# Turning attention probabilities by halves of 64 queries on two row halves of TensorE

## The reference, cut to what matters

```python
def masked_softmax(s, mask):
    s = jnp.where(mask, s, NEG)
    p = jax.nn.softmax(s, axis=-1)
    return jnp.where(mask, p, 0.0)

s = jnp.einsum('bhqd,bhkd->bhqk', qi, kh).astype(jnp.float32) * scale
s = s + ci[..., None] - c_h[:, :, None, :]
p = masked_softmax(s, key_pos[None, :] <= t[:, None])
return jnp.einsum('bhqk,bhkd->bhqd', p.astype(vh.dtype), vh)
```

## Time and profile before

| | |
|---|---|
| median of 3 runs | 1459.34 us (1457.41 to 1459.77) |
| the profiled execution: time | 1457.6 us |
| its span | 1455.8 us |
| TensorE busy | 1423.5 us, 98% |
| weight loads (beside TensorE) | 924.4 us, 63% |
| VectorE busy | 936.0 us, 64% |
| ScalarE busy | 859.1 us, 59% |
| fox loop and nsa loop | from 976 to 1015 us and from 1260 to 1407 us of the span |

### The profile page before, as it was taken

How to read it: one execution, slowest core, us unless ns; L and a number is a source line. 1 busy time by engine, 2 the same in 40 slices (tenths; PEclk the granted TensorE clock), 3 DMA queues, 4 the chain that set the end, 5 groups by cost and what they waited for, 6 DMA issues and landing times.

```text
span 1455.8 us, 24918 instructions
## 1 busy us (share of the span) xinstructions
PE 1423.5 (98%) x10148; PEld 924.4 (63%) x10148; DVE 936.0 (64%) x2086; ACT 859.1 (59%) x1184; POOL 64.9 (4%) x151
## 2 busy tenths in 40 slices
PE   7999999999999999999999999999999999899998
PEld 4444477555568548667588874746695855466677
DVE  6731565888688666555677624578667336788864
ACT  6654356777654765454473554557655557677863
POOL 0000000000000100000010000100100000000000
PEclk9999999999999999999999999999999999999999
DMA  6333322223232433333332333230223433200002
GB/s 194 97 106 100 103 87 88 66 76 120 75 128 89 142 108 102 129 126 102 102 101 75 117 93 111 89 116 3 67 88 116 137 105 98 72 2 1 2 4 99
DMA packets 128563, 132.32 MB, mean 91 GB/s; under 512 B 9961, under 2 KB 125329, under 8 KB 128321
## 3 DMA queue, kind: packets, MB, share of 16 engines
q1 hardware_dynamic: 126000, 121.56, 26.1%
q0 software_dynamic: 2448, 9.17, 1.9%
HBM read 128.58 MB, written 2.10 MB: 90 GB/s over the span
## 4 chain that ended last, share of the span: by engine, by line
PE 90%; DVE 4%; ACT 3%; issue 1%; DMA 1%; SPq 0%; POOL 0%; DVEq 0%; ACTq 0%
PE bank L740 14%; PE bank L742 14%; PE bank L741 14%; PE bank L793 8%; PE bank L795 8%; PE bank L794 8%; PE bank L992 3%; PE bank L1009 3%; PE bank L975 3%; DVE wring L1987 1%; PE bank L919 1%; PE bank L937 1%; PE bank L971 1%; PE bank L1167 1%; PE bank L873 1%
## 5 line engine op out<-in xcount | busy, mean ns | idle before, releaser
L740 PE MATMUL bank<-xT,whigh 128*128 128x512 f16 x952 | 360.8, 379 | 1.6 <-DVE wring L1987 1.6
L741 PE MATMUL bank<-xT,whigh 128*128 128x512 f16 x952 | 360.8, 379 | 0.0
L742 PE MATMUL bank<-xT,wring 128*128 128x512 f16 x952 | 360.8, 379 | 0.0
L1987 DVE SCALAR_TENSOR_TENSOR wring<-wring,wsc,whigh 128x2048 f16<-128x2048 f32 (+2 forms) x106 | 245.2, 2313 | 136.1 <-ACT whigh L1356 135.5
L1356 ACT ACTIVATE whigh<-wring,wsc 128x2048 f16<-128x2048 f32 (+2 forms) x106 | 209.0, 1972 | 108.8 <-DVE wsc L1890 88.2
L1373 ACT ACTIVATE whigh<-wring 128x2048 bf16<-128x2048 f32 (+2 forms) x106 | 199.1, 1878 | 91.2 <-DMA wring<-in_w_down 26.9
L793 PE MATMUL bank<-whigh,slab 128*128 128x256 f16 x800 | 218.0, 273 | 1.8 <-DVE wring L1987 1.3
L795 PE MATMUL bank<-whigh,slab 128*128 128x256 f16 x800 | 218.0, 273 | 0.0
L794 PE MATMUL bank<-wring,slab 128*128 128x256 f16 x800 | 218.0, 273 | 0.0
L740 PEld LDWEIGHTS bank<-xT,whigh 128*128 128x128 f16 x952 | 93.4, 98 | 113.8 <-issue 2.7
L742 PEld LDWEIGHTS bank<-xT,wring 128*128 128x128 f16 x952 | 93.1, 98 | 112.3
(11 more groups left out here) (333 smaller groups left out, 2245.3 us busy)
## 6 DMA issues: line engine op xcount, KB each, us to landing
wring<-in_w_in SPq DMA_DIRECT2D x27, 1024.0 KB, 5.1
wring<-in_w_up SPq DMA_DIRECT2D x16, 1024.0 KB, 5.4
wring<-in_w_down SPq DMA_DIRECT2D x16, 1024.0 KB, 5.1
wring<-in_even_w_in SPq DMA_DIRECT2D x14, 1024.0 KB, 5.3
wring<-in_odd_w_in SPq DMA_DIRECT2D x14, 1024.0 KB, 5.1
wring<-in_w_a SPq DMA_DIRECT2D x4, 1024.0 KB, 5.3
wring<-in_w_out SPq DMA_DIRECT2D x4, 1024.0 KB, 5.1
wring<-in_even_w_out SPq DMA_DIRECT2D x4, 1024.0 KB, 5.1
```

The costliest lines, as they stand in the source:

```text
L740: pe.matmul(bank, wh[:, k, wcol:wcol + width], xh[:, k, :], start=k == 0, stop=False)
L741: pe.matmul(bank, wh[:, k, wcol:wcol + width], xl[:, k, :], start=False, stop=False)
L742: mm = pe.matmul(bank, wl[:, k, wcol:wcol + width], xh[:, k, :], start=False, stop=k == KC - 1)
L1987: dve.scalar_tensor_tensor(low_of(i)[:, :, 0:m], loaded(i)[:, :, 0:m], wsc[:, n:n + 1], high_of(i)[:, :, 0:m], ALU.mult, ALU.subtract).the ...
```

## The change

For every block of 128 queries by 128 keys, two transposes stand where one stood. Each takes 64 queries: half k = 0 on partitions 0 to 63, half k = 1 on 64 to 127, with the 64x64 corner of the identity on the same partitions. Half k goes to bank `TPB[k]`, where the blocks of both heads follow each other in pieces of 64 columns; before, each head had its bank. ScalarE's copy puts them in order, so that `xT` holds for each head all 128 queries of a block side by side. A head's part begins at e times the step's width, no longer at a multiple of 512. TensorE waits once for the scaling of both heads, where it waited for each in turn.

```diff
-        def turned_probs(i, e):
-            return xT[:, 2 * (i % TURNED_SLOTS) + e, :]
+        def turned_pair(i, w):
+            return xT[:, 2 * (i % TURNED_SLOTS):2 * (i % TURNED_SLOTS) + 2, :].rearrange("p a n -> p (a n)")[:, 0:2 * w]
+
+        def turned_probs(i, e, w):
+            return turned_pair(i, w)[:, e * w:e * w + w]
...
+                        pe.wait_ge(s_(n + "_pn"), n_(n + "_pn", 2 * s + 2))
+                        w = width(steps[s][2])
                         for e in range(2):
-                            pe.wait_ge(s_(n + "_pn"), n_(n + "_pn", 2 * s + e + 1))
-                            for j in range(width(steps[s][2]) // P):
-                                mm = pe.transpose(TPB[e][:, j * P:(j + 1) * P], probs(s, e, SEQ)[:, j * P:(j + 1) * P], ident[:, :])
+                            for j in range(w // P):
+                                for k in range(2):
+                                    rows = slice(k * HD, k * HD + HD)
+                                    c = (e * w + j * P) // 2
+                                    mm = pe.transpose(TPB[k][:, c:c + HD], probs(s, e, SEQ)[rows, j * P:(j + 1) * P], ident[rows, rows])
...
-                                    mm = pe.matmul(ob[e][:, t * P:(t + 1) * P], A.v(2 * m + e, b, j), turned_probs(s, e)[:, c + j * P:c + (j + 1) * P],
+                                    mm = pe.matmul(ob[e][:, t * P:(t + 1) * P], A.v(2 * m + e, b, j), turned_probs(s, e, width(parts))[:, c + j * P:c + (j + 1) * P],
...
-                        c = 2 * (s % TURNED_SLOTS)
                         act.wait_ge(s_(n + "_tp"), n_(n + "_tp", s + 1))
-                        act.activation(xT[:, c:c + 2, 0:w], bank[:, 4:6, 0:w], ACT.Copy).then_inc(s_(n + "_te"), 1)
+                        act.activation(turned_pair(s, w).rearrange("p (x k q) -> p k x q", k=2, q=HD), bank[:, 4:6, 0:w].rearrange("p k (x q) -> p k x q", q=HD), ACT.Copy).then_inc(s_(n + "_te"), 1)
```

## The result

The changed kernel took 1441.57 us (median of four runs, 1440.65 to 1445.17) against 1459.52 for the kernel before in the same comparison. The two medians lie 17.95 us apart. The ratio of the runs is .9887, with a 95% interval from .9875 to .9900: faster by 16.5 us, between 14.6 and 18.2. Forecast were 1440.0 and 17.9 us less, with a range from 1435 to 1450.5.

The account below looks back on a forecast made before the run. TensorE's own work was taken to pace the NSA loop, VectorE next. Savings of 15.8 (NSA) + .5 (FOX) + 1.0 + .6 (tails) = 17.9 us took the profiled 1457.6 to 1439.7, stated as 1440.0 us; range 1435 to 1450.5.

Parts of the forecast that it names:

- A pair at .06 us, the load longer than the stream: Transposes on TensorE: two overlapping halves cost .06 us (load .06, stream .05) against .11, saving 2.0 us per six steps.
- The Trainium skill's rule by columns alone: Rival on transpose loads: 128 columns load in about 107 ns, a pair stays at .11 us, 1450 us in all; chance .08.
- (c): Whether TensorE can issue a pair's four records in 60 ns: yes, at 16 ns per matmul; left out of the sum.
- .15 us per step for the array's division: Pause between scores and transposes on TensorE: goes when both use 64x128, saving .15 us per step, .9 per six.
- TensorE at 14.8, VectorE at 15.3, with coupling 15.5: Six NSA steps: TensorE falls from 17.7 to 14.8 us, VectorE becomes the bound at 15.3, uneven iterations make it 15.5.
- The coupling of .2: NSA loop: .2 us added per six steps for uneven iterations and score buffers for two steps only.
- NSA, 15.8 us: NSA loop, 43 steps from score to score: 7.2 × (17.7 − 15.5) = 15.8 us saved.
- FOX loop, .5 us: Whole FOX loop: .5 us saved, VectorE being busy 8.19 of TensorE's 8.34 us per three steps.
- Tails, 1.0 and .6 us: After the last scores: 20 pairs of half transposes in FOX save 1.0 us, 12 in NSA save .6.
- the copy and the single wait at 0: ScalarE's reordering copy in runs of 64 and TensorE's one wait for both heads: each costs 0.

Follow-up runs that it names:

- e4: Kernel before the change, with VectorE's scaling of head 1 of each pair left out: 1458.55 us, ratio 1.0002 to the kernel before.
- e5: Changed kernel with both transposes of a block on row half 0 (queries 0 to 63), queries 64 to 127 left out: 1456.31 us, ratio .9983.
- e3: Changed kernel with VectorE's scaling of head 1 of each pair left out: 1436.46 us, ratio .9852 to the kernel before.
- e9: Changed kernel once more, unedited, with more rounds: 1442.55 us, ratio .9890 to the kernel before.
- e1: Changed kernel with its transposes alone undone, the reordering copy and the single wait kept: 1458.04 us, ratio 1.0000 to the kernel before.
- e2: Changed kernel with the transposes' two inner loops exchanged, all of one row half first for each head: 1441.54 us, ratio .9885 to the kernel before.
- e10: As e6, but GpSimd takes up the NSA low halves before waiting for the third weight slice of the output projection: 1440.66 us, ratio .9872.
- e6: Changed kernel with the attention outputs' low halves, all but each layer's last, made by GpSimd instead of VectorE: 1472.78 us, ratio 1.0088 to the kernel before.
- e7: Changed kernel with small idle products of constants before TensorE's waits in loop starts and the NSA tail: 1444.29 us, ratio .9898 to the kernel before.

## Why the prediction was right, point by point

The path was right: TensorE alone set the pace before (e4), the overlap of the halves made the gain (e5), and VectorE took over (e3). That the forecast gain of 17.9 us meets the 17.95 between the medians so closely is luck. The ratio gives 16.5, and the same kernel beside other runs of the kernel before was 15.6 us under their median (e9). The clock, and two terms that were off, make more difference than that.

- *A pair at .06 us, the load longer than the stream*: .06 in the timeline, and e5 shows that the overlap is what makes it. Reading a transpose's load against the loads of 64 and of 128 ordinary columns gave it. That the load is what sets .06 over the stream's .05 is inferred: in e5 a half with its load takes .062 on one row half, with half as many instructions in that time. The Trainium skill's rule by columns alone ("TensorE: Matmul & The Clock Gate", section "LDWEIGHTS (loading the stationary operand)") would have left the pair at about .11, an estimate, and the trace disagrees. The 62 ns per matmul that the prediction weighs in (c) are given for hardware decode off; the 16 ns of the earlier trace rows and the .06 of a pair show that they do not apply to these runs, not that they are wrong.
- *.15 us per step for the array's division*: the size is confirmed by e5, .9 per six steps; the reason is argued. The Trainium skill says ("TensorEngine Tiling (Array Packing)", section "Key Properties") that changing the tiling mode drains TensorE. The trace agrees: the pause was there between 64x128 and 128x128 and is gone between 64x128 and 64x128. The price here is .15 us with the load that is exposed.
- *TensorE at 14.8, VectorE at 15.3, with coupling 15.5*: 14.88 (e3), and 15.45 in the changed kernel. The coupling of .2 was a choice between 0 and 1.0, and that it came so close (.15 over VectorE's sum) is luck in part.
- *NSA, 15.8 us*: from step 4's scores to step 47's 127.6 us before, 112.3 in e9's profile: 15.3. In the first profile 12.5, since the clock fell in the loop's first steps.
- *FOX loop, .5 us*: the term was too small for the stage. Steps 4 to 11 took 19.43 us before and 17.92 in e9 (19.38 in the first profile, with the fall of the clock). I had judged from one stretch of three steps, in which VectorE was busy 8.19 of 8.34 us. The whole loop before reads:

```profile
986.13:1005.56 19.43, 19.43 (x196) 13.49 (x197) 18.38 (x78) 17.10 (x46) 0.00 (x0) 1.00 0.01 3
```

  With 18.38 of 19.43 us, VectorE had a good microsecond free there.
- *Tails, 1.0 and .6 us*: NSA's is right where the clock held (9.82 us before, 9.21 in e9). FOX's was too large: from the last scores to the last values it was 8.56 us before (1005.56 to 1014.12) and 8.31 after (1004.95 to 1013.26). The transposes are shorter, but once VectorE sets the pace the last exponentials come later after their scores, and ScalarE's copies stand behind them. In the tail of the changed kernel TensorE waits for such a copy:

```profile
1011.19 0.59 PE L999 MATMUL bank<-ident,scr 64*128 64x64 f32 x12 [1.09 <-ACT xT L1698]
```

- *The rest*: the copy and the single wait at 0 (e1). With e9's stages the sum is 15.3 + 1.5 + .6 + .25 = 17.6 against 17.9. The two wrong terms, +1.0 and −.75, nearly cancelled, which is luck.

The stages gained 17.6 us, but the span of e9's profile is only 15.9 us under the one before. Nothing of what FOX gave reached the NSA loop there. From the first FOX scores to the first NSA scores, before and in e9:

```profile
976.46:1259.95 283.49, 276.92 (x2022) 181.04 (x2022) 173.13 (x390) 176.24 (x255) 15.01 (x31) 0.99 0.28 88
976.25:1259.76 283.51, 274.49 (x2103) 179.45 (x2103) 173.15 (x390) 176.06 (x255) 15.01 (x31) 0.99 0.28 88
```

The 1.7 us that FOX had won went into the fall of the clock at 1246.72. It is no wait that swallows them whatever the kernel: in e3, which has no fall there, the same distance is 279.8 us (its FOX loop is shorter still).

What no step of the prediction had is the clock. It fell in the loop starts, before (once, at 980.7 us) and after, at different places; in the tail the first profile has it too, which the traces before the change do not. There TensorE is busy 8.88 of 9.82 us before and 7.49 of 9.21 after. Five profiles of kernels with the short loop (after, e2, e3, e9, e10) show it in the tail three times. That the change makes such falls likelier is argued from this, not shown. Where they fall explains the 3.5 us between the two profiles of the changed kernel: 5.8 in the three stretches, less 1.7 before the NSA loop and some .5 in small differences.

## What to carry to other kernels

Before costing a faster instruction, sum up the next engine's work over one period of the loop, over the whole loop and not its fullest stretch: here 2.2 of TensorE's 2.8 us came through, because VectorE stood at 15.3. Two half transposes on the two row halves cost .06 us against .11 for the whole one, and they share the division of the array with score products that contract over 64 rows, which saves another .15 us per step. Before giving work to an idle engine, look at what stands ahead of it in that engine's program: e6 won in the loop and lost 32 us at a wait in front of the moved work. And follow a gain from its stage to the end of the span before adding it up: FOX's 1.7 us were won and lost again in the same profile.

## What the runs showed of the hardware

- Half transposes on two row halves overlap even when they come in fours: sixteen take .64 us, against .59 when they alternate (e2) and 1.09 when all are on one half (e5), each until the values begin.
- An f32 transpose's load of 128 columns has records of 144 ns on 64 rows and 140 on 128, against 194 for an ordinary f32 load. As 64 ordinary columns are worth 58 ns (194 less 136), the transpose's 128 are worth about 60, an estimate; e5's .062 us for each half with its load allows no more.
- GpSimd takes 2.9 us for a 128x512 product and subtraction that VectorE does in .66. Of VectorE's instructions beside it one per pair is longer, .76 us for .48, the one that spans the change between GpSimd's two (e10).
- In two executions of the same code the granted clock fell to 1.2 GHz in different places. The price hangs on the place: 1.5 and 2.8 us in the full steps of FOX and NSA, 1.7 before the NSA loop, but .2 in the first steps of a loop, where TensorE mostly waits. Idle products kept the clock up in the three stretches aimed at and won nothing (e7).
